# Ten expert weight pieces in idle buffers outside the ring, and a norm scale moved from rows to the copies out of PSUM

## The chip, the cores and the metric

One core of a Trainium2 chip runs the whole program as one launch. The metric is device microseconds (us) of one execution. TensorE (PE) does the matmuls and transposes, VectorE (DVE) and ScalarE (ACT) the elementwise work, GpSimd (POOL) a little of it and most of the small DMAs, and the queue of SyncE (SP) issues every weight transfer.

## The reference, cut to what matters

Everything is fp32, 512 tokens of width 1024. A first block (attention of two kinds, then a mixture of 32 experts) ends in a norm, and a second block of two layers begins with another norm of the same rows:

```python
def rmsnorm(x, g):                       # rms_norm is the same
    return x * rsqrt(mean(x * x, -1) + EPS) * g

h2 = rmsnorm(x, norm_ffn_g)              # first block, second half
for e in range(32):                      # every token takes 2 of 32 experts of one group
    hid = silu(h2 @ w_gate[e]) * (h2 @ w_up[e])
    m += (hid @ w_down[e]) * combine[:, e:e + 1]
x = rmsnorm(x + m, final_norm_g)         # end of the first block

h = rms_norm(x, norm_gain[0])            # second block, layer 0
cols = h @ w_in_a                        # q, k, v (3 x 3072), q_mem (512), gate (1536)
# q and k are normed for each head of 128, v is used as it is, silu(gate)
mem_out = cross attention of q_mem (normed) over kv = rmsnorm(mem) @ w_mem_kv[0]
```

Two row scales are thus applied one after the other: `both_rs[:, 0:4]` (final norm) and the second norm's, and `n2_rs` is their product, one number for each token. A scale of a row of x is also a scale of the same row of x @ w.

## The kernel before, in words

**Weights.** All weights come as `pieces` of up to 128x1024 fp32 (512 KB), in one fixed order. SP's `load(p)` (L633) puts piece p into slot p % 6 of the ring `wraw` once the low half of piece p - 6 has been made (L635). ACT's `feed(p)` (L864) copies it into a rounded high half `whi` (L869; the slot is one of four, and free when piece p - 4 has been used), DVE's `feed(p)` makes the low half `wlo` = raw - high (L1434), and PE multiplies in three passes (high by high, high by low, low by high), six matmuls of up to 512 columns for each token tile and piece. All engines run programs written out by hand; semaphores tie them together, and each engine works strictly in its own order.

**Experts.** Pieces P0, P1, ... (counted from `P_MOE`) are those of the experts: four gate/up pieces and two down pieces for each of 32 experts, 192 in all, in the order gate/up of expert n, then down of expert n - 1. Tokens are gathered group by group (eight groups of four experts, 128 rows each) by an indirect DMA of POOL (`gather`, L779), transposed (`columns`), multiplied (`gate_up` L2561, `down` L2584), added to the gathered rows (`expert_sums`, L1876) and scattered back (L790). Ahead of it come the router's logits, ranks and `slot_from`, which the first gather waits for (DVE, L1786 to L1846). DVE makes the low half of the last piece before the experts (`after(CH["out1"])`) in the middle of that routing, and SP's load of P5 waits for it.

**The end of the first block.** PE puts the last group's rows back with `last_mm` (L2650, eight products of 512 columns, two PE instructions each), DVE adds them to x1 (`x_sum`, L1933) and multiplies a copy by the final gain (`x_gain`, L1935, into `xn`), ACT squares both (L1261), DVE and ACT make the scales (L1937 to L1943), and DVE (three tiles, L1946) and ACT (one, L1267) write the scaled rows into x1. PE transposes x1 (`memory_stage`, L2238), in an order that puts token 4p + r at column p of tile r. ACT and DVE split the transposed rows into `AT_hi` and `AT_lo`. PE's `memory_stage(0)` runs four tiles of `mkv01` (values of the memory, which don't need x) before it waits for the scaled rows and four among the transposes, then `qm0` (q_mem, four pieces by four tiles, 96 matmuls), the head norms' transposes and the memory attention. POOL multiplies `xn` by the final scale and writes it to `x_mid` for the residual (L814, L815).

**Layer 0 of the second block.** For each of eight heads (`hd`) three chunks q, k, v of 384 columns run beside the attention of the head before, step by step (i = 0 to 11). At the end of a q or k chunk, for each of four tiles: ACT squares the PSUM bank (L1307), DVE sums the squares (L2007) and multiplies the bank by the head gain (L2009), which frees the bank for PE's next chunk; ACT's next square waits for DVE's sum. A v chunk is copied out by ACT (L1303), and the gate goes through Silu (L1028).

Of the kernel before, what the change touches and what calls it, by code (L numbers as in the profile page):

```python
# [20 lines left out]
ALU = mybir.AluOpType  # L21
# [83 lines left out]
def build(nc, A, out):  # L105
    ctx = ExitStack()
    with ctx:
# [29 lines left out]
        x_mid2 = nc.dram_tensor("x_mid2", (T, D), F32, kind="Internal").ap()  # L137

# [37 lines left out]
        gains = take(64)  # L176
        g_moe = gains[:, 53:61]
# [117 lines left out]


# [41 lines left out]
        raw_in = [S(f"raw_in{i}") for i in range(RAW)]  # L338
        hi_done = S("hi_done")
# [64 lines left out]
        sqrt_ready = stat(1)  # L404
        far_at = stat_at[0]
# [30 lines left out]
        before, iota_g, iota_s, empty, tok1 = (const(k, c_moe, C_BASE) for k in ("before", "iota_g", "iota_s", "empty", "tok1"))  # L436
        h2T = take(4096, KD, T)
# [21 lines left out]
        fin_g = take(D)  # L459
        big = take(4096)  # L460
# [19 lines left out]
        put = take(T)  # L480
        gen_sil = take(1024, 2, T)
# [18 lines left out]
        assert mem_at >= moe_top  # L500
        memx = [view(mem_at, 2048, 2, D), take(2048, 2, D)]
# [125 lines left out]
        @block.sync  # L627
        def _(sp):
            for t in range(NT):
                sp.dma_start(xr[:, t, :], A["x"][0, t * P:t * P + P, :]).then_inc(S(f"x_in{t}"), 16)  # L630

            def load(p):
                loads, per, n = pieces[p]  # L633
                if p >= RAW:
                    sp.wait_ge(lo_done[(p - RAW) % SPL], (p - RAW) // SPL + 1)  # L635
                dst = wraw[:, p % RAW, 0:per * n].rearrange("p (k n) -> p k n", k=per)
                share = 96 // len(loads)
                for c0, w, src in loads:
                    sp.dma_start(dst[:, :, c0:c0 + w], src).then_inc(raw_in[p % RAW], share)

            for p in range(NP):
                load(p)

        NORMS = (("n1", 4, 0, 0), ("cq", 4, 0, 0), ("ckv", 4, 0, 0), ("mem0", 2, 2, 0), ("ffn", 8, 0, 0),
                 ("n2", 8, 4, 0), ("km0", 0, 8, 2), ("qm0", 0, 0, 4), ("mem1", 2, 2, 0), ("n3", 4, 4, 0), ("km1", 0, 8, 2),
# [5 lines left out]
        def so_far(name, what, n):  # L653

            return sum(row[what] for row in NORMS[:ORDER.index(name)]) + n

# [31 lines left out]
        def _(pool):  # L688
# [64 lines left out]
            for p in BESIDE_PICKS:  # L753
                pool.wait_ge(hi_done, p + 1)
                pool.tensor_tensor(w_slot(wlo, p, p % SPL), w_slot(wraw, p, p % RAW), w_slot(whi, p, p % SPL).bitcast(F32),
                                   ALU.subtract).then_inc(lo_done[p % SPL], 1)
# [53 lines left out]

            pool.wait_ge(norm_rt, ORDER.index("n2") + 1)
            pool.wait_ge(norm_xs, so_far("n2", 2, NT))
# [46 lines left out]
        def _(act):  # L859
            his = [0]  # L860

            def feed(p):

                if p >= NP:  # L864
                    return
                act.wait_ge(raw_in[p % RAW], 96 * (p // RAW + 1))
                if p >= SPL:
                    act.wait_ge(piece_used, p - SPL + 1)
                act.activation(w_slot(whi, p, p % SPL), w_slot(wraw, p, p % RAW), ACT.Copy).then_inc(hi_done, 1)  # L869
# [8 lines left out]
            def evac(name, dst, func=ACT.Copy, scale=1.0, fed=False, rows=None):  # L878
# [4 lines left out]
                for t in range(chunks[j]["nt"]):  # L883
# [5 lines left out]
                    act.activation(d, src, func, scale=scale if rows is None else ns[rows]["rs"][:, t:t + 1]).then_inc(acc_free[t], 1)  # L889
# [14 lines left out]
            def tb(name, i):  # L904
                return TP[(TPU[name] + i) % 2]
# [94 lines left out]
            def memory_stage(l):  # L1000
# [3 lines left out]
                for k in range(KD):  # L1004
                    hi(name, k, AT_hi[:, k, :], tb(name, k), g_n2[l][:, k:k + 1])
                    if k % 2:
                        feed(chunks[j]["first"] + k // 2 + SPL)
                evac(f"mkv{l}1", lambda t: vm[l][:, t, :], fed=True)
                head_norm(f"km{l}", f"mkv{l}0", km_tok[l], 2, ns[f"km{l}"], msq)
                evac(f"qm{l}", lambda t: qm_tok[:, t, :])  # L1010
# [6 lines left out]
            def gate_out(l, c, tmp):  # L1017

                j = CH[f"gate{l}{THIRDS[l][c]}"]
                for t in range(NT):  # L1020
# [7 lines left out]
                    act.activation(tmp[n % len(tmp)], ACC[t][:, :], ACT.Silu).then_inc(acc_free[t], 1)  # L1028
# [10 lines left out]
            for at, src in ((0, A["norm_mix_g"][0]), (8, A["mla_q_norm_g"][0]), (11, A["mla_kv_norm_g"][0]), (13, A["norm_ffn_g"][0]),  # L1039
                            (21, A["norm_gain_2"][0]), (29, A["norm_gain_2"][1]), (37, A["mem_norm_gain_2"][0]),  # L1040
                            (45, A["mem_norm_gain_2"][1])):
# [10 lines left out]
            act.activation(gains[:, 0:53], SC[0][:, 0:53], ACT.Copy).then_inc(S("gains_ready"), 1)  # L1052
# [203 lines left out]
            done = so_far("n2", 1, 0)  # L1256
            for t in range(NT):
                for what, src, ss in (("x_sum", x1[:, t, :], fin_ss), ("x_gain", xn[t], n2_ss)):
                    act.wait_ge(S(what), 2 * t + 2 if what == "x_sum" else t + 1)
                    act.wait_ge(norm_ss, done)  # L1260
                    act.activation(junkD, src, ACT.Square, accum_out=ss[:, t:t + 1]).then_inc(norm_ss, 1)  # L1261
                    done += 1
# [3 lines left out]
            act.wait_ge(S("n2_rs"), 1)  # L1266
            act.activation(x1[:, 3, :], xn[3], ACT.Copy, scale=n2_rs[:, 3:4]).then_inc(norm_xs, 1)  # L1267
# [7 lines left out]
            for hd in range(9):  # L1275
                for i in range(12):
# [1516 lines left out]
```

## Time and profile before

| | |
|---|---|
| three runs | 2171.64, 2175.24, 2175.42 us, median 2175.24 |
| the profiled execution | 2176.21 us, of which the span is 2174.4 us |
| TensorE | 93% busy, mean granted clock 0.976 |
| chain that ended last | PE 71%, DVE 12%, ACT 8%, DMA 5%, issue 3% |
| DMA | 255.46 MB, mean 117 GB/s |

The span is what the profile covers, from the first to the last instruction. A matmul's end is modelled, so neighbouring matmuls overlap in the lists; the distance from start to start is their pace. A table row in square brackets ends with the idle time before the group and what ended it.

### The profile page before, as it was taken

What the parts mean: (1) busy time and instruction counts of PE and PEld (TensorE: products, weight loads), DVE (VectorE), ACT (ScalarE), POOL (GpSimd) and SP (SyncE); (2) the same over time, 40 slices, a digit from 0 to 9 for tenths busy, and PEclk for the clock granted to TensorE, in tenths of its full rate; (3) what the DMA queues carried; (4) which work ended last, traced back from release to release, by engine and by line L of the source; (5) the groups of instructions that cost most, each with busy time, mean ns of one, the idle gap of its engine ahead of it and who ended that gap; (6) DMA issues with size and microseconds to landing.
All of it is one profiled execution on the core that took longest, in us unless ns stands there. A gap on an engine that the chain in (4) does not pass through costs nothing.

```text
span 2174.4 us, 28065 instructions
## 1 busy us (share of the span) xinstructions
PE 2020.1 (93%) x10543; PEld 1707.1 (79%) x10543; DVE 1175.6 (54%) x2428; ACT 1032.7 (47%) x1705; POOL 243.7 (11%) x345
## 2 busy tenths in 40 slices
PE   7999999999899997799999999999999899998988
PEld 7977667777777775699988898888777677877877
DVE  3344387454899997454344334443433546736752
ACT  4644433344778786553444344434432554344430
POOL 0611132011010100212120112111000000000000
PEclk9999999999999999899999999999999999999999
DMA  4411121143899998322222222222243312112120
GB/s 141 134 47 40 58 70 57 39 146 140 284 373 362 373 368 309 97 63 74 66 72 59 73 66 66 66 74 86 68 129 116 116 55 78 30 49 78 49 88 39
DMA packets 177985, 255.46 MB, mean 117 GB/s; under 512 B 13557, under 2 KB 92218, under 8 KB 177850
## 3 DMA queue, kind: packets, MB, share of 16 engines
q1 hardware_dynamic: 168832, 221.33, 31.3%
q0 software_dynamic: 8768, 31.81, 4.0%
q8 instruction: 85, 1.39, 0.3%
q10 hardware_dynamic: 250, 0.52, 0.1%
q14 instruction: 50, 0.41, 0.1%
HBM read 239.45 MB, written 14.16 MB: 117 GB/s over the span
## 4 chain that ended last, share of the span: by engine, by line
PE 71%; DVE 12%; ACT 8%; DMA 5%; issue 3%; ACTq 0%; SPq 0%; POOL 0%; DVEq 0%; POOLq 0%
PE pb L2212 51%; DVE wlo L1434 5%; PE pb L2240 5%; DMA wraw<-w_down 5%; ACT whi L869 3%; PE pb L2744 3%; PE pb L2676 2%; PE pb L2292 2%; PE pb L2667 2%; PE pb L2305 1%; PE pb L2561 1%; PE pb L2584 1%; PE pb L2448 1%; PE pb L2753 1%; PE pb L2256 1%
## 5 line engine op out<-in xcount | busy, mean ns | idle before, releaser
L1434 DVE TENSOR_TENSOR wlo<-wraw,whi 128x1024 fp32r<-128x1024 f32 (+4 forms) x436 | 497.6, 1152 | 588.4 <-ACT whi L869 585.1
L2212 PE MATMUL pb<-whi,AT_hi 128*128 128x512 f32 (+4 forms) x1992 | 768.4, 386 | 22.7 <-ACT arena L889 5.8
L2212 PE MATMUL pb<-whi,AT_lo 128*128 128x512 f32 (+4 forms) x1992 | 730.8, 367 | 0.0
L2212 PE MATMUL pb<-wlo,AT_hi 128*128 128x512 f32 (+4 forms) x1992 | 730.2, 367 | 0.0
L869 ACT ACTIVATE whi<-wraw 128x1024 fp32r<-128x1024 f32 (+4 forms) x452 | 446.5, 996 | 477.3 <-PE pb L2212 403.6
L2212 PEld LDWEIGHTS pb<-whi,AT_hi 128*128 128x128 f32 x1992 | 380.4, 191 | 97.8 <-issue 44.3
L2212 PEld LDWEIGHTS pb<-whi,AT_lo 128*128 128x128 f32 x1992 | 378.7, 190 | 46.1
L2212 PEld LDWEIGHTS pb<-wlo,AT_hi 128*128 128x128 f32 x1992 | 380.7, 191 | 39.1 <-issue 2.5
L2240 PE MATMUL pb<-arena 128*128 128x128 f32 (+1 forms) x1180 | 188.9, 288 | 48.3 <-ACT arena L902 15.4
L2240 PEld LDWEIGHTS pb<-arena 128*128 128x128 f32 (+1 forms) x1180 | 147.8, 149 | 89.4 <-ACT arena L902 23.2
L2561 PE MATMUL pb<-whi,AT_hi 128*128 128x512 f32 x256 | 104.2, 407 | 4.3 <-DVE wlo L1434 2.3
L2561 PE MATMUL pb<-wlo,AT_hi 128*128 128x512 f32 x256 | 101.3, 396 | 0.0
L2561 PE MATMUL pb<-whi,AT_lo 128*128 128x512 f32 x256 | 100.8, 394 | 0.0
L2744 PEld LDWEIGHTS pb<-arena 128*128 128x128 f32 x576 | 78.4, 201 | 18.1 <-issue 10.7
L2744 PE MATMUL pb<-arena 128*128 128x64 f32 (+2 forms) x576 | 82.0, 290 | 10.7 <-DVE arena L2124 4.2
L1374 ACT ACTIVATE arena<-arena 128x512 f32<-128x512 f32 x64 | 40.3, 631 | 92.1 <-DVE arena L2110 74.8
L957 ACT ACTIVATE arena<-pb,small 128x64 f32<-128x64 f32 x64 | 20.1, 314 | 115.2 <-PE pb L2305 115.2
L902 ACT ACTIVATE arena<-pb 128x512 f32<-128x512 f32 (+2 forms) x102 | 55.3, 574 | 35.9 <-PE pb L2240 35.9
L703 POOL TENSOR_TENSOR arena<-arena 128x64 f32<-128x64 f32 (+3 forms) x41 | 18.3, 446 | 461.1 <-DVE small L2021 300.4
L2584 PE MATMUL pb<-whi,AT_hi 128*128 128x512 f32 x128 | 52.6, 411 | 16.7 <-DVE AT_lo L1868 13.0
L1283 ACT ACTIVATE arena<-arena,small 128x768 f32<-128x768 f32 x32 | 30.0, 939 | 66.9 <-DVE small L1982 66.9
L2561 PEld LDWEIGHTS pb<-whi,AT_hi 128*128 128x128 f32 x256 | 48.8, 191 | 14.7 <-DVE wlo L1434 3.0
(302 smaller groups left out, 2313.2 us busy)
## 6 DMA issues: line engine op xcount, KB each, us to landing
wraw<-w_in_a SPq DMA_DIRECT2D x288, 128.0 KB
wraw<-w_gate SPq DMA_DIRECT2D x128, 256.0 KB
wraw<-w_up SPq DMA_DIRECT2D x128, 256.0 KB
wraw<-w_down SPq DMA_DIRECT2D x64, 512.0 KB
wraw<-w_in_b SPq DMA_DIRECT2D x40, 512.0 KB
wraw<-w_in SPq DMA_DIRECT2D x28, 512.0 KB
wraw<-w_mem_kv SPq DMA_DIRECT2D x16, 512.0 KB
wraw<-w_in_a SPq DMA_DIRECT2D x16, 512.0 KB
```

The lines of the kernel that those rows point to most:

```text
L869: act.activation(w_slot(whi, p, p % SPL), w_slot(wraw, p, p % RAW), ACT.Copy).then_inc(hi_done, 1)
L902: act.activation(dst, src, ACT.Copy, scale=scale).then_inc(tp_free[u % 2], 1)
L1374: act.activation(kq[n % 5], kq[n % 5], ACT.Exp).then_inc(S("gl_x"), 1)
L1434: dve.tensor_tensor(w_slot(wlo, p, p % SPL), w_slot(wraw, p, p % RAW), w_slot(whi, p, p % SPL).bitcast(F32), ALU.subtract).then_inc(lo_don ...
L2212: mm = pe.matmul(ACC[t][:, 0:n], a, b, start=kc == 0 and q == 0, stop=i == c["count"] - 1 and kk == per - 1 and q == 2)
L2240: tr = pe.transpose(TP[u % 2][0:b.shape[1], at:at + P], b, ident)
L2292: pe.matmul(SC[U % 2][:, 0:u["kw"]], u["q"], u["k"], start=True, stop=True).then_inc(att_s, 1)
L2561: mm = pe.matmul(ACC[n % 2].rearrange("p (w f) -> p w f", w=2), a, b, start=k == 0 and m == 0, stop=k == 7 and m == 2)
L2584: mm = pe.matmul(ACC[2 + i], x, y, start=e == 0 and b == 0 and q == 0, stop=e == 3 and b == 1 and q == 2)
L2667: mm = pe.matmul(dst[:, 0:k.shape[1]], q, k, start=True, stop=True)
L2676: mm = pe.matmul(D_OUT, d_pt[:, P * b:P * b + P], v, start=b == 0, stop=b == 5)
L2744: mm = pe.matmul(dst, tile(k, s), rhs, start=True, stop=True)
```

## The change

(1) Pieces P6 to P15 (`HELD`) don't go into the ring: each has a buffer of its own, in regions of the arena that are unused until after the experts, and a semaphore of its own. Their loads wait for events that come before P5's load; the ring counts on without them, so P16 takes the slot that P6 had. (2) PE transposes x1 as it is after `x_sum`, beside the last `mkv01` tiles; the final gain is folded into the gain column of the transposed rows (`g_n2[0]`, DVE, once at the start, from one more small load). The squares and the scales are made beside it. `n2_rs` goes through DRAM (one write and one read of 512 numbers by POOL) to come back as `rs_perm` in the order of the transposed tiles, and every copy out of PSUM of layer 0 that reads x's columns takes it as its scale: `qm0` (ACT), the squares and the v copies (ACT), the product with the head gain (DVE, now `scalar_tensor_tensor`) and the Silu (ACT).

```diff
+        NHELD = 10
+        HELD = range(P_MOE + RAW, P_MOE + RAW + NHELD)
+        ring_at = lambda p: p if p < HELD.start else p - NHELD
+        ring_piece = lambda r: r if r < HELD.start else r + NHELD
...
+        held = [view(at + 1024 * i, 1024) for at, n in ((mem_at + 2304, 2), (gen_at, 2), (big_at + 2048, 2), (h2_at, 4)) for i in range(n)]
...
-                if p >= RAW:
-                    sp.wait_ge(lo_done[(p - RAW) % SPL], (p - RAW) // SPL + 1)
+                if p in HELD:
+                    i = p - HELD.start
+                    if i == 0:
+                        sp.wait_ge(S("y_sum"), 2 * NT)
+                    elif i == 2:
+                        sp.wait_ge(norm_ss, so_far("mem0", 1, 2))
+                    elif i == 4:
+                        sp.wait_ge(norm_ss, so_far("ffn", 1, 8))
+                    elif i == 6:
+                        sp.wait_ge(S("rt_mm"), 1)
+                elif ring_at(p) >= RAW:
+                    before = ring_piece(ring_at(p) - RAW)
+                    sp.wait_ge(lo_done[before % SPL], before // SPL + 1)
...
+            pool.wait_ge(S("n2_rs"), 1)
+                pool.dma_start(rs_rows.rearrange("(t p) -> p t", p=P), n2_rs).then_inc(S("rs_out"), 16)
+                pool.wait_ge(S("rs_out"), 16)
+                pool.dma_start(rs_perm, rs_rows.rearrange("(p r) -> p r", r=4)).then_inc(S("rs_back"), 16)
             pool.wait_ge(norm_rt, ORDER.index("n2") + 1)
-            pool.wait_ge(norm_xs, so_far("n2", 2, NT))
...
+                if l == 0:
+                    during(CH["qm0"])
+                    act.wait_ge(S("rs_back"), 16)
+                evac(f"qm{l}", lambda t: qm_tok[:, t, :], fed=l == 0, row_scale=None if l else rs_perm)
...
+            square_of(0)
+            square_of(1)
+            for k in range(KD):
+                hi("n2", k, AT_hi[:, k, :], tb("n2", k), g_n2[0][:, k:k + 1])
+                if k in (1, 3):
+                    feed(chunks[j]["first"] + k // 2 + SPL)
+                if k == 5:
+                    for t in range(2):
+                        wait_acc(act, j, t)
+                        act.activation(vm[0][:, t, :], ACC[t], ACT.Copy).then_inc(acc_free[t], 1)
+                        feed(chunks[j]["first"] + 2 + t + SPL)
+            for n in range(2, 8):
+                square_of(n)
...
-                                act.activation(v2[:, hd % 2, t, :], ACC[t][:, 0:384], ACT.Copy).then_inc(acc_free[t], 1)
+                                act.activation(v2[:, hd % 2, t, :], ACC[t][:, 0:384], ACT.Copy, scale=rs_perm[:, t:t + 1]).then_inc(acc_free[t], 1)
...
-                                act.activation(sqb, ACC[t][:, 0:384], ACT.Square).then_inc(S("qk_sq"), 1)
+                                act.activation(sqb, ACC[t][:, 0:384], ACT.Square, scale=rs_perm[:, t:t + 1]).then_inc(S("qk_sq"), 1)
...
-            for t in range(3):
-                dve.tensor_scalar(x1[:, t, :], xn[t], n2_rs[:, t:t + 1], None, ALU.mult).then_inc(norm_xs, 1)
...
-                            dve.tensor_tensor(qk_t[:, t, :].rearrange("p (g c) -> p g c", g=3),
...
+                            dve.scalar_tensor_tensor(qk_t[:, t, :].rearrange("p (g c) -> p g c", g=3),
+                                                     ACC[t][:, 0:384].rearrange("p (g c) -> p g c", g=3), rs_perm[:, t:t + 1],
+                                                     qkg[:, :, i // 4, :], ALU.mult, ALU.mult).then_inc(acc_free[t], 1)
...
-            memory_stage(0, lambda t: x1[:, t, :], lambda bank, t: bank.rearrange("p (r t q) -> p t q r", t=NT, r=4)[:, t], 4)
+                if t:
+                    project_tile("mkv01", (t - 1) // 2, (t - 1) % 2)
+            project_tile("mkv01", 1, 1)
+            pe.wait_ge(S("x_sum"), 8)
...
+            n2_t(0)
+            n2_t(1)
+            for s in range(4):
+                project_tile("mkv01", 2 + s // 2, s % 2)
+                n2_t(2 + s)
+            for i in range(4):
+                ready("n2", (2 * i, 2 * i + 1))
+                for t in range(NT):
+                    project_tile("qm0", i, t)
+                    if i == 0 and t % 2:
+                        n2_t(6 + t // 2)
+            memory_attention(0)
```

DVE's order becomes: all `x_sum` adds, the eight low halves of the transposed rows, then the four `x_gain` products and the scales.

## Rows read from the trace of the kernel before

**Rows 1.** The page: GB/s of all DMA in 40 slices of 54.4 us.
```profile
GB/s 141 134 47 40 58 70 57 39 146 140 284 373 362 373 368 309 97 63 74 66 72 59 73 66 66 66 74 86 68 129 116 116 55 78 30 49 78 49 88 39
```

**Rows 2.** Timeline of SP's queue, 530 to 562: start, duration, engine, line, operation.
```profile
537.15 0.35 SPq L639 DMA_DIRECT2D wraw<-w_gate  x1
541.31 0.35 SPq L639 DMA_DIRECT2D wraw<-w_gate  x1
```

**Rows 3.** Waits, 575 to 598, longest first: us in total, times, longest.
```profile
ACT whi L869 <- PE pb L2561: 1.7, 6, 0.3
```

**Rows 4.** Waits, 540 to 900.
```profile
ACT whi L869 <- DMA wraw<-w_up: 20.0, 21, 2.7
PE pb L2584 <- DVE AT_lo L1868: 13.0, 15, 2.7
ACT whi L869 <- DMA wraw<-w_down: 10.1, 29, 1.8
```

**Rows 5.** Timeline of POOL: scatters of the first and second group.
```profile
599.73 1.17 POOL L790 DMA_INDIRECT x_moe<-arena  x1 [56.23 <-DVE arena L1876]
636.57 1.71 POOL L790 DMA_INDIRECT x_moe<-arena  x1 [28.70 <-DVE arena L1876]
```

**Rows 6.** The chain that ended last, in order of time, 500 to 960: start, us, what.
```profile
540.65 5.87 DMA arena<-x_all,arena
...
602.33 6.75 DMA wraw<-w_down
...
892.58 23.41 PE pb L2212 x96
```

**Rows 7.** DMA issues, 675 to 685: us from issue to landing.
```profile
arena<-x_all,arena POOLq DMA_INDIRECT x1, 8.2
```

**Rows 8.** Timeline of PE, 855 to 935: start, duration, and idle time before.
```profile
860.30 7.14 PE L2650 MATMUL pb<-arena 128*128 128x512 f32 x16 [1.71 <-DVE arena L1908]
...
876.89 1.12 PE L2238 MATMUL pb<-arena 128*128 128x128 f32 x4 [4.00 <-DVE arena L1946]
...
892.58 0.77 PE L2212 MATMUL pb<-whi,AT_hi 128*128 128x512 f32 x1 [2.30 <-ACT arena L889]
...
915.82 0.60 PE L2240 MATMUL pb<-arena 128*128 128x128 f32 x4
```

**Rows 9.** A window of 5 us: busy us of PE, PEld, DVE, ACT, POOL; clock, DMA.
```profile
875.00:880.00 5.00, 3.11 (x10) 2.63 (x11) 2.59 (x4) 1.60 (x2) 2.85 (x1) 0.50 0.00 0
```

**Rows 10.** Timeline of DVE and ACT, 855 to 935.
```profile
870.43 1.22 DVE L1935 TENSOR_TENSOR arena<-arena 128x1024 f32<-128x1024 f32 x1
...
874.56 0.16 DVE L1943 TENSOR_TENSOR small<-small 128x4 f32<-128x4 f32 x1 [0.62 <-ACT small L1265]
...
871.76 1.06 ACT L1261 ACTIVATE arena<-arena 128x1024 f32<-128x1024 f32 x1
...
916.02 0.60 ACT L889 ACTIVATE arena<-pb 128x512 f32<-128x512 f32 x1 [0.76 <-PE pb L2212]
```

**Rows 11.** DMA issues of POOL: KB each, us from issue to landing.
```profile
arena<-const POOLq DMA_DIRECT2D x1, 134.5 KB, 2.4
arena<-lb_logits POOLq DMA_DIRECT2D x2, 4.0 KB, 4.3
...
x_mid<-arena POOLq DMA_DIRECT2D x4, 512.0 KB, 3.7
```

**Rows 12.** Groups of ACT by form: busy us, mean ns; a source `small` is a scale column.
```profile
L1303 ACT ACTIVATE arena<-pb 128x384 f32<-128x384 f32 x32 | 15.7, 492 | 18.4 <-PE pb L2212 18.4
L889 ACT ACTIVATE arena<-pb,small 128x384 f32<-128x384 f32 x8 | 4.3, 581 | 0.6 <-PE pb L2212 0.6
```

**Rows 13.** Waits of PE, 947 to 1500.
```profile
PE pb L2676 <- DVE arena L1989: 9.0, 7, 1.3
PE pb L2667 <- ACT arena L1303: 5.3, 7, 0.8
```

**Rows 14.** Timeline, the first 22 us: the gains' transpose.
```profile
9.84 0.32 PE L2374 MATMUL pb<-arena 53*128 53x53 f32 x1 [9.84 <-DMA arena<-mem_norm_gain]
```

More of the change, by code:

```diff
@@ L338, in build @@
         raw_in = [S(f"raw_in{i}") for i in range(RAW)]
+        raw_held = [S(f"raw_held{i}") for i in range(NHELD)]
         hi_done = S("hi_done")
@@ L404, in build @@
         sqrt_ready = stat(1)
+        rs_perm = stat(4)
         far_at = stat_at[0]
@@ L624, in build, with so_far @@
         block = ctx.enter_context(nc.Block())
+        NORMS = (("n1", 4, 0, 0), ("cq", 4, 0, 0), ("ckv", 4, 0, 0), ("mem0", 2, 2, 0), ("ffn", 8, 0, 0),
+                 ("n2", 8, 0, 0), ("km0", 0, 8, 2), ("qm0", 0, 0, 4), ("mem1", 2, 2, 0), ("n3", 4, 4, 0), ("km1", 0, 8, 2),
+                 ("qm1", 0, 0, 4))
+        ORDER = [n[0] for n in NORMS]
+        norm_ss, norm_ms, norm_rt, norm_xs = S("norm_ss"), S("norm_ms"), S("norm_rt"), S("norm_xs")
+        head_sq, head_red = S("head_sq"), S("head_red")
+        def so_far(name, what, n):
+            return sum(row[what] for row in NORMS[:ORDER.index(name)]) + n
         @block.sync
@@ L876, in after, with evac @@
                 feed(chunks[j]["first"] + chunks[j]["count"] - 1 + SPL)
-            def evac(name, dst, func=ACT.Copy, scale=1.0, fed=False, rows=None):
+            def evac(name, dst, func=ACT.Copy, scale=1.0, fed=False, rows=None, row_scale=None):
                 j = CH[name]
@@ L888, in evac @@
                         src = src.rearrange("p (h c) -> p h c", h=d.shape[1])
[L889 removed]
+                    if rows:
+                        row_scale = ns[rows]["rs"]
+                    act.activation(d, src, func, scale=scale if row_scale is None else row_scale[:, t:t + 1]).then_inc(acc_free[t], 1)
                 if not fed:
@@ L1027, in gate_out @@
                         act.wait_ge(S("gated0"), n - 1)
-                    act.activation(tmp[n % len(tmp)], ACC[t][:, :], ACT.Silu).then_inc(acc_free[t], 1)
+                    act.activation(tmp[n % len(tmp)], ACC[t][:, :], ACT.Silu, scale=1.0 if l else rs_perm[:, t:t + 1]).then_inc(acc_free[t], 1)
             def gated_hi(l, c):
@@ L1254, in _, with square_of @@
                     act.activation(gen_sil[:, 1, :], ACC[1], ACT.Silu).then_inc(S("gen_silu"), 1)
[L1256 to L1262, printed above, removed]
+            def square_of(n):
+                t = n % NT
+                src, ss = ((x1[:, t, :], fin_ss), (xn[t], n2_ss))[n // NT]
+                act.wait_ge(S("x_gain"), t + 1) if n >= NT else act.wait_ge(S("x_sum"), 2 * t + 2)
+                act.wait_ge(norm_ss, so_far("n2", 1, n))
+                act.activation(junkD, src, ACT.Square, accum_out=ss[:, t:t + 1]).then_inc(norm_ss, 1)
+            j = CH["mkv01"]
+            square_of(0)
+            square_of(1)
+            for k in range(KD):
+                hi("n2", k, AT_hi[:, k, :], tb("n2", k), g_n2[0][:, k:k + 1])
+                if k in (1, 3):
+                    feed(chunks[j]["first"] + k // 2 + SPL)
+                if k == 5:
[5 more added lines that the diff above has]
+                square_of(n)
             act.activation(sqrt_ready, ns["ffn"]["ms"][:, 0:1], ACT.Sqrt)
@@ L1599, in memory_stage @@
                 j = CH[f"mkv{l}1"]
-                for k in range(KD):
+                for k in range(KD) if l else ():
                     lo(name, k, AT_lo[:, k, :], tb(name, k), AT_hi[:, k, :], g_n2[l][:, k:k + 1])
@@ L1933, in _ @@
                     dve.tensor_tensor(x, LAST[(2 * t + i) % 4], x, ALU.add).then_inc(S("x_sum"), 1)
+            j = CH["mkv01"]
+            for k in range(KD):
+                lo("n2", k, AT_lo[:, k, :], tb("n2", k), AT_hi[:, k, :], g_n2[0][:, k:k + 1])
+                if k in (1, 3):
+                    feed(chunks[j]["first"] + k // 2 + SPL)
+                if k == 5:
+                    for q in (2, 3):
+                        feed(chunks[j]["first"] + q + SPL)
+            for t in range(NT):
                 dve.wait_ge(S("x_sum"), 2 * t + 2)
@@ L2328, in memory_stage, with memory_rows @@
             def memory_stage(l, rows, place, before):
+                if l:
+                    memory_rows(l, rows, place, before)
+                memory_attention(l)
+            def memory_rows(l, rows, place, before):
                 name = f"n{l + 2}"
```

70 lines of the change are left out of this document (39 added, 31 removed).

## The prediction

> **What bounds the kernel now.** I read the chain of waits in order of time first, then the GB/s slices, then waits and timelines of three stretches. In the expert stage (552 to 860 us) the slices show 362 to 373 GB/s [rows 1], and the chain runs over weight transfers and over the gather that opens the stage [rows 6]. ACT waits 30.1 us for weights (20.0 + 10.1), of which some reaches PE: it stands 13.0 us ahead of the down products for their split input [rows 4]. That looks like a stage that wants more prefetch. But from 575 to 598 us, the time of the first group of experts, the longest of ACT's waits for a copy is on PE, and no DMA is in the list's head [rows 3]: the weights fall behind only afterwards. Around 870 us the stage's end is bound by latency: PE stands 4.00 us for DVE's scaled rows, runs at half clock (0.50 in 875 to 880), and stands 2.30 us more for ACT's copy of the mkv01 banks [rows 8, 9]. Layer 0's heads are PE's own work, except at the end of a q chunk, where PE waits for DVE 7 times, 9.0 us in all, and at v, where it waits for ACT's copies 7 times, 5.3 us [rows 13].
>
> **The held pieces.** P5 is issued at 537.15 and P6 at 541.31, four us later, when P0's low half is made [rows 2]. With the change P6 to P15 go out right behind P5: 5.2 MB, some 13 us at 400 GB/s, done by about 552. What follows is the point: P16 to P21 then fill the six ring slots, at the times at which P6 to P11 were loaded before, and P22 has to wait for the low half of P16, which is not made before about 578 us, after all held pieces are used. Between those times SP has nothing to issue. So the lead isn't carried: at 578 us the ring is full, in place of nearly full, and from there every load is released by the same low halves as before. The first group had no wait for weights anyway [rows 3]. The second group's wait is a load issued at 602.33 that takes 6.75 us [rows 6], well after the ring is back in its old rhythm. Groups come 36.84 us apart (599.73 to 636.57) [rows 5]; I give the held pieces -0.5 us, with 0 and -2 as ends for the second group.
>
> They cost something at the start. The first gather (issued 540.65) is on the chain and lands after 5.87 us with hardly a weight transfer beside it [rows 6]. Now ten pieces are in the queues at that moment. A gather in the full stage takes up to 8.2 us [rows 7]. That is 0 to +2.3 us on the chain, since PE does nothing else before its transposes; I take +1.4.
>
> **The end of the first block.** Before: last_mm starts at 860.30, qm0's 96 matmuls start at 892.58 and take 23.24 us to 915.82, the last copy of qm0 ends at 916.62 (916.02 + 0.60) [rows 8, 10]. After, on PE: last_mm 7.14; the eight mkv01 tiles of six matmuls, at qm0's full-clock pace of 0.227 us each (21.8 us for 96; the first few ran at half clock), 1.36 each, 10.9; six groups of transposes at 0.4, 2.4. That is 880.8. There PE waits for bank 0: ACT must split row 5 and copy the bank, about 1.6 us. Then qm0 21.8 and two transposes 0.8: PE is done at about 905.0, 10.8 us earlier. The 4.00 and most of the 2.30 us are gone and, without the long idle time, the half clock too.
>
> What is late next is the scale. ACT and DVE finish the eighth row's split at about 891; ACT then squares the remaining six (last two of them behind DVE's products), and the last square ends at about 898. From the last square's start to n2_rs takes 2.8 us before (871.76 to 874.56) [rows 10], so n2_rs is ready at about 899.6, 25 us later than before. Then come two DMAs in series. Nearest rows: a write to DRAM in this very stretch, 3.7 us for 512 KB; a load of 4 KB as single numbers, 4.3 us; the quickest of POOL, 2.4 us for 134.5 KB [rows 11]. I take 3.7 for the write and 4.3 for the read, as the nearest in kind, and 0.4 for POOL's and ACT's wakeups: rs_perm is there at 908.0. ACT's four copies (0.69 with a scale column, 0.1 overlapped) end at 910.4. That is 6.2 us before 916.62. What is queued behind ACT's wait is the last feed and the copies of the keys' transposes, and PE waits for those; they follow the copies as before. With 2.4 us for each DMA the copies are bound by PE and end at about 907.2 (-9.4); with 8.2 us, the slowest issue shown [rows 7], they end at 918.8 (+2.2). After 905 PE idles as it did before 924, so the half clock moves more than it goes: -0.5, ends -2 and +1. Together -6.7. DVE's and ACT's scaled rows (four) go with this; POOL's x_mid products start after its two DMAs, at about 904, take 15 us and are covered by the attention, which before ends at 946.
>
> The Trainium skill, "DMA: Bandwidth & Descriptors", section on the two cost components, gives a DMA a fixed cost of about 2.0 us and next to nothing for few bytes. By that rule the two would take 4.0 in place of 8.0 us, rs_perm would be there at 904, before PE is done, and this part would give about -9.9. The rows here, all above 2.4, don't bear that out for POOL's transfers, but they carry other traffic in front of them.
>
> **The scale column in layer 0.** The copy of a bank with a scale column takes 581 ns where one without takes 492, at 384 columns [rows 12]: +0.089 us for each. Where does it stand on the path? At the end of a q chunk PE reaches the next chunk and then the probabilities' product, which waits for DVE 7 times [rows 13]; that DVE work stands behind ACT's four squares, each released by DVE's sum of the one before, so a square's length adds in full: 4 x 0.089 = 0.36 for each of 7 heads, 2.5 us. At the end of a k chunk the squares start as soon as the first tile is complete and PE has a product to do first, so I count nothing; if they bind there too it is 8 x 0.36 = 2.9 more. v: PE waits for the last copy, 8 x 0.09 = 0.7. The gate's Silu, three chunks, 0.3. DVE's product grows too, from tensor_tensor to scalar_tensor_tensor; no row has it at 384 columns with a column scale from a PSUM bank, and I bound it by 0 and by 0.1 us a tile; it runs beside ACT's next square and is covered except for the last tile. Sum +3.5, ends 0 and +7.
>
> **The start.** PE's transpose of the gains waits for the last small load at 9.84 [rows 14]; one more load is issued ahead of it, 0.4 us by the spacing of the others, and x itself comes just behind. +0.3, ends 0 and +0.6. DVE's product of gains lies in idle time.
>
> **Sum.** -0.5 + 1.4 - 6.7 + 3.5 + 0.3 = -2.0. The profiled execution took 2176.21 us, the median is 2175.24; 2.0 less than the median is 2173.2. A difference under 0.2% (4.35 us) is about what a measurement of this kernel can't tell from none.
>
> **Rivals.**
> *The loads keep their lead.* If the ring's starvation is inherited from the cold start, the ten pieces take away most of what reaches PE, 13.0 less the 5 us of the last group, where x's return shares the DMA: -8. For it: the stage sits at its transfer rate [rows 1]. Against: the first group shows no such wait. 2173.2 - 7.5 = 2166.
> *The scale comes quickly.* Both DMAs near 2 us: -3.2 more, 2170, just outside "same".
> *The scale comes slowly (slower).* Place: ACT's wait for rs_back ahead of qm0's copies. Numbers of four bytes into DRAM and back, behind ACT, PE and then the whole attention. Price: every us beyond 905 + 3 of rs_perm; it decides from about 10 us for the two on (the part's gain is then no more than the 4.7 that the rest costs), and at 8.2 each the part is +1.7 in place of -6.7: 2173.2 + 8.4 = 2181.6.
> *The column binds everywhere (slower).* Squares at k as well and DVE's longer product in the chain: +3.5 more, with the gather at +2.3: 2178.
>
> **Chances.** The forecast 0.45, with its own range 2170.5 to 2177; quick scale 0.20; lead kept 0.12; slow scale 0.12; column everywhere 0.11. The range from 2165 to 2181 takes in the first four in most of their spread. Faster by over 0.2%: lead kept, most of quick scale and the forecast's edge, 0.36. Slower: slow scale and a part of the last case, 0.19. Same: 0.45.
>
> **What would show it.** SP's queue: ten loads between 538 and 550, then none between about 562 and 577; a first gather of 6.5 to 8 us; scatters still near 37 us apart, the first at 600 to 602. PE: qm0 starts near 883 without idle time of 4 us, at full clock. ACT: an idle stretch of a few us ahead of the first qm0 copy, released by a DMA, at about 908. L1307 at 580 ns, and 7 waits of L2676 each 0.3 us longer. It is wrong if scatters come under 36 us apart, if no wait for rs_back is seen, or if the heads' stage is not 2 to 5 us longer.

## The result, and the profile after

The changed kernel took 2180.82 us (median of 9, 2178.95 to 2188.01); the kernel before, beside it, 2175.24 (2171.16 to 2179.32). The ratio is 1.0034, 95% interval 1.002 to 1.0048: slower by some 7 us, where 2.0 us faster, 2173.2, was forecast (the two medians themselves are 5.6 us apart). The profiled execution took 2180.32 us, span 2178.6.

SP's queue does what the prediction said of it [rows 2]. Timeline of SP, after, 530 to 580:
```profile
537.95 0.65 SPq L687 DMA_DIRECT2D arena<-w_gate  x1
...
542.76 0.92 SPq L687 DMA_DIRECT2D arena<-w_down  x2
...
557.43 1.86 SPq L687 DMA_DIRECT2D wraw<-w_down  x2
575.49 0.35 SPq L687 DMA_DIRECT2D wraw<-w_gate  x1
```
The held pieces (written to `arena`) are all issued by 544, the ring is refilled by 559, and then nothing is issued for 16 us. What ACT and PE wait for in the stage is what it was [rows 4]. Waits, after, 540 to 900:
```profile
ACT whi L910 <- DMA wraw<-w_up: 19.5, 20, 2.8
PE pb L2659 <- DVE AT_lo L1930: 12.9, 15, 2.7
ACT whi L910 <- DMA wraw<-w_down: 10.7, 31, 1.5
```
The first gather is slower, 8.37 us against 5.87 [rows 6]. The chain and the timelines of PE and POOL, after:
```profile
537.72 8.37 DMA arena<-x_all,arena
```
```profile
546.14 1.98 PE L2308 MATMUL pb<-arena 128*128 128x128 f32 x8 [5.30 <-DMA arena<-x_all,arena]
```
```profile
598.60 1.17 POOL L827 DMA_INDIRECT x_moe<-arena  x1 [58.03 <-DVE arena L1938]
...
635.52 1.71 POOL L827 DMA_INDIRECT x_moe<-arena  x1 [28.59 <-DVE arena L1938]
```
The groups still come 36.9 us apart [rows 5]. At the end of the first block PE does what was forecast: no wait of 4.00 us, full granted clock in 875 to 880 where it was 0.50 [rows 8, 9], and it is done at 905.44 (forecast 905.0). The window of 5 us, and PE's timeline, after:
```profile
875.00:880.00 5.00, 5.00 (x30) 4.24 (x29) 4.01 (x5) 3.61 (x5) 0.00 (x0) 1.00 0.27 79
```
```profile
882.56 0.47 PE L2280 MATMUL pb<-whi,AT_hi 128*128 128x512 f32 x1 [1.36 <-ACT arena L1322]
...
905.44 0.60 PE L2308 MATMUL pb<-arena 128*128 128x128 f32 x4
918.27 5.15 PE L2308 MATMUL pb<-arena 128*128 128x128 f32 x20 [12.23 <-ACT arena L945]
```
Then it stands 12.23 us. ACT's copies wait 10.63 us for `rs_perm`, and POOL, which may issue the read only when the write has landed, stands 9.43 us for that. DVE, POOL and ACT, after:
```profile
898.85 0.16 DVE L2014 TENSOR_TENSOR small<-small 128x4 f32<-128x4 f32 x1 [0.62 <-ACT small L1328]
```
```profile
899.31 0.78 POOL L850 DMA_DIRECT2D rs_rows<-small  x1 [65.63 <-DVE small L2014]
909.51 0.54 POOL L852 DMA_DIRECT2D small<-rs_rows  x1 [9.43 <-DMA rs_rows<-small]
```
```profile
914.79 2.42 ACT L932 ACTIVATE arena<-pb,small 128x512 f32<-128x512 f32 x4 [10.63 <-DMA small<-rs_rows]
```
The copies end at 917.21 (914.79 + 2.42), against 916.62 before [rows 10]. The transfers' own list (us from issue to landing at the end) and a window of 6 us inside the wait:
```profile
x_mid<-arena POOLq DMA_DIRECT2D x4, 512.0 KB, 3.0
rs_rows<-small POOLq DMA_DIRECT2D x1, 2.0 KB, 9.9
small<-rs_rows POOLq DMA_DIRECT2D x1, 2.0 KB, 5.3
```
```profile
899.00:905.00 6.00, 6.00 (x29) 4.95 (x28) 4.73 (x15) 3.39 (x6) 0.78 (x1) 1.00 0.03 0
```
2 KB take 9.9 us while the DMA engines are 3% busy (last but one number) and move 0 GB/s; 512 KB to DRAM take 3.0 us a little later. So the 9.9 us aren't other traffic.

In layer 0, ACT's squares are as long as priced [rows 12], and PE's waits stand elsewhere than I put them [rows 13]. Groups of ACT by form, and waits of PE, 947 to 1500, after; the last line is the one of the kernel before that belongs to the last line of after:
```profile
L1368 ACT ACTIVATE arena<-pb,small 128x384 f32<-128x384 f32 x64 | 37.1, 580 | 45.9 <-DVE small L2075 34.2 <-PE pb L2280 11.6
L1364 ACT ACTIVATE arena<-pb,small 128x384 f32<-128x384 f32 x32 | 18.6, 582 | 16.4 <-PE pb L2280 16.4
```
```profile
PE pb L2771 <- DVE arena L2057: 8.9, 7, 1.3
PE pb L2762 <- ACT arena L1364: 6.0, 7, 0.9
PE pb L2280 <- DVE arena L2077: 1.8, 7, 0.3
```
```profile
PE pb L2212 <- DVE arena L2009: 0.4, 1, 0.4
```

To compare runs, whose start differs by up to 6 us before anything changed, I read four stretches off POOL's timeline of each profiled execution. A runs from the first gather's issue to the first scatter, and B from the first to the seventh scatter (most of the expert stage). C runs from the seventh scatter to POOL's first product of layer 0's k heads with their norm's scale; the block's end and the q and k chunks of the first head lie in it. D runs from there to POOL's eighth such product (seven heads). In us; "time" is the ratio to the kernel before, where it was timed:

| kernel | A | B | C | D | time |
|---|---|---|---|---|---|
| before | 59.1 | 223.3 | 163.1 | 494.3 | 1 |
| after | 60.9 | 224.5 | 163.0 | 497.9 | 1.0034 |
| e1 held pieces alone | 62.4 | 223.7 | 162.9 | 494.2 | 1.0013 |
| e2 norm's move alone | 59.5 | 224.6 | 164.1 | 497.8 | 1.0043 |
| e3 product, no transfers | 61.1 | 225.0 | 156.9 | 497.9 | 1.0006 |
| e4 no column on q, k | 60.6 | 226.3 | 163.4 | 495.0 | 1.0034 |
| e5 16-byte write | 61.1 | 224.1 | 155.2 | 497.8 | |
| e6 ACT's queue | 62.4 | 222.5 | 162.7 | 497.8 | |
| e7 held after the gather | 57.1 | 224.6 | 164.7 | 497.8 | 1.0010 |
| e8 repaired, nothing held | 59.5 | 223.8 | 154.4 | 495.0 | 0.9963 |
| e9, e13 spaced numbers | 62.7, 62.3 | 225.5, 224.4 | 154.3, 154.2 | 497.8 | 0.9993 (e13) |
| e10 8-byte write | 60.8 | 224.0 | 160.1 | 497.9 | |
| e11 = e8 + held late | 57.0 | 223.4 | 153.4 | 495.1 | 0.9959 |
| e12 = e11, 16-byte write | 57.2 | 223.9 | 154.5 | 495.0 | 0.9968 |
| e14 = e11, spaced numbers | 57.1 | 224.9 | 152.2 | 495.0 | 0.9945 |

D repeats within 0.1 us among kernels that don't differ there, A and C within some 2 us; B (222.5 to 226.3) follows none of the edits. The three kernels that hold nothing have a mean B of 223.9, the thirteen with held pieces 224.4. e5, e6, e9 and e10 are single executions, read for their traces and not for their time.

### The profile page after: what moved, and what is told of

Its sections match the earlier page's. It is cut to its first block, busy times and chain, and to the rows that moved or that the text cites. A ratio compares the mean times of both kernels' runs of the same rounds, so it can differ in the third digit from the quotient of the medians.

```text
span 2178.6 us, 28064 instructions
## 1 busy us (share of the span) xinstructions
PE 2016.2 (93%) x10543; PEld 1702.7 (78%) x10543; DVE 1176.3 (54%) x2426; ACT 1040.6 (48%) x1704; POOL 242.9 (11%) x347
## 4 chain that ended last, share of the span: by engine, by line
PE 70%; DVE 13%; ACT 8%; DMA 6%; issue 2%; ACTq 0%; SPq 0%; POOL 0%; DVEq 0%; POOLq 0%
PE pb L2280 50%; DVE wlo L1495 6%; DMA wraw<-w_down 5%; PE pb L2308 5%; ACT whi L910 3%; PE pb L2839 2%; PE pb L2771 2%; PE pb L2360 2%; PE pb L2762 2%; PE pb L2373 1%; PE pb L2659 1%; PE pb L2636 1%; PE pb L2523 1%; PE pb L2848 1%; ACT arena L945 1%
## 5 line engine op out<-in xcount | busy, mean ns | idle before, releaser
L1495 DVE TENSOR_TENSOR wlo<-wraw,whi 128x1024 fp32r<-128x1024 f32 (+4 forms) x426 | 484.7, 1148 | 581.5 <-ACT whi L910 577.9
L910 ACT ACTIVATE whi<-wraw 128x1024 fp32r<-128x1024 f32 (+4 forms) x442 | 435.9, 994 | 458.7 <-PE pb L2280 387.1
L2280 PEld LDWEIGHTS pb<-whi,AT_hi 128*128 128x128 f32 x1992 | 379.2, 190 | 99.6 <-issue 44.3
L1632 DVE COPY arena<-pb 128x128 f32<-128x128 f32 (+3 forms) x64 | 31.4, 491 | 52.7 <-PE pb L2308 52.1
```

Source lines behind the costliest of these rows:

```text
L910: act.activation(w_slot(whi, p, p % SPL), raw_slot(p), ACT.Copy).then_inc(hi_done, 1)
L1495: dve.tensor_tensor(w_slot(wlo, p, p % SPL), raw_slot(p), w_slot(whi, p, p % SPL).bitcast(F32), ALU.subtract).then_inc(lo_done[p % SPL], 1)
L2280: mm = pe.matmul(ACC[t][:, 0:n], a, b, start=kc == 0 and q == 0, stop=i == c["count"] - 1 and kk == per - 1 and q == 2)
```

## The experiments

**Each part alone.** e1 is the kernel before with `HELD` and the addresses of its pieces; e2 is the changed kernel with
```
-        NHELD = 10
+        NHELD = 0
```


> The kernel before with the ten held pieces alone, its norm as it was. My reading of the changed kernel: the held pieces cost the first gather (PE stood 5.3 us for it in place of 2.8, the stage began about 1.8 us later against its input) and give nothing back, since the queue of loads stands still from 560 to 575: +1.8 us, 2177.0; scatters 36.9 us apart. Rival A (the lead is worth something, and the slower end hides it): below 2173, scatters under 36.7 us apart. Rival B (the gather's delay is taken back by a later, fuller ring): 2175.2, no difference.

Measured: 2175.79 us, ratio 1.0013 (1.0000 to 1.0025); wait for the gather 5.37 us. A costs 3.3 us here, 1.8 in the changed kernel, and B, which varies by more than that from kernel to kernel, shows nothing given back, here or in the means. The first rival has nothing for it; the second isn't excluded by the time, but A and B don't bear its mechanism out.

> The changed kernel with no held pieces (their number set to 0), the norm's scale still on the PSUM copies. If the two parts add up: start +0.7, end of the first block -0.6, the heads' stage +4.1, some 2179.4, and the first gather's wait is 2.8 us again. Rival (the parts work on each other: held pieces or their loads are what makes the round trip of the scale through memory slow): the write of the 512 numbers takes under 5 us and the time falls to 2175. My theory has that write at 9 us or more here too.

Measured: 2182.15 us, 1.0043 (1.0030 to 1.0056); wait for the gather 3.25 us, and the write still holds POOL 9.6 us. The held pieces have no part in the slow write. The two parts' losses (0.13% and 0.43%) add up to more than the whole's 0.34%, but within the intervals.

**The scale without the transfers.** e3 puts this in the place of both DMAs (`of_four` and `in_four` are 0/1 masks summed from `ident`):
```
+            dve.tensor_tensor(spread_rs.rearrange("p (t j) -> p t j", t=NT), n2_rs.unsqueeze(2).broadcast_to([P, NT, 32]),
+                              of_four.unsqueeze(1).broadcast_to([P, NT, 32]), ALU.mult).then_inc(S("n2_rs"), 1)
...
+                        pe.matmul(SC[1][:, 0:4], spread_rs, in_four, start=True, stop=True).then_inc(S("rs_mm"), 1)
...
+                    act.activation(rs_perm, SC[1][:, 0:4], ACT.Copy).then_inc(S("rs_back"), 1)
```


> The changed kernel, but the scale gets to its new layout on the chip: DVE spreads the four columns over 128 (times a 0/1 mask), one TensorE product with a second 0/1 mask gives [128,4], ACT copies it. No transfer. Theory (the round trip of 512 four-byte numbers is the step that ate the gain): the scale is there at about 902, qm0's copies end at 905 to 906 in place of 917.2, all that follows moves up by some 11.5 us: 2169. Rival A (something else binds right behind, the preparation of layer 0's heads by POOL's loads or the attention's start): copies end at 906 but the heads begin less than 5 us earlier: 2176 or more. Rival B (my forecast's own size, 6.7 us in all against the kernel before): 2175.

Measured: 2174.86 us, 1.0006 (0.9996 to 1.0015), C 6.1 us shorter than in the changed kernel. The copies start 46.0 us after last_mm's start in place of 54.4, and what they wait for is no longer a transfer; ACT's timeline in e3:
```profile
902.73 0.21 ACT L953 ACTIVATE small<-small 128x8 f32<-128x8 f32 x1 [2.13 <-DVE small L1523]
902.84 2.30 ACT L905 ACTIVATE whi<-wraw 128x768 fp32r<-128x768 f32 x3
905.05 0.15 ACT L1052 ACTIVATE small<-pb 128x4 f32<-128x4 f32 x1
905.23 2.42 ACT L927 ACTIVATE arena<-pb,small 128x512 f32<-128x512 f32 x4
```
ACT reaches the copies only after the keys' norm and three weight pieces. The theory named the right step and took too much for it: what comes next is work on ACT and DVE. Part of that is the edit's own. The keys' root (L953) comes 43.5 us after last_mm's start, 41.4 in the changed kernel, since DVE's work ahead of it is longer in e3: the spread takes 1.13 us, and the keys' small operation takes 1.34 us where it took 0.17 (DVE in e3):
```profile
897.87 1.13 DVE L2014 TENSOR_TENSOR arena<-small,arena 128x128 f32<-128x128 f32 x1
...
901.35 1.34 DVE L1523 TENSOR_SCALAR small<-small 128x8 f32<-128x8 f32 x1
```

**Why the round trip is slow.** e5, e6, e9 and e10 are each an edit of the changed kernel's two DMAs. e5 has the write contiguous in each partition and the read scattered:
```
-                pool.dma_start(rs_rows.rearrange("(t p) -> p t", p=P), n2_rs)
+                pool.dma_start(rs_rows.rearrange("(p t) -> p t", p=P), n2_rs)
-                pool.dma_start(rs_perm, rs_rows.rearrange("(p r) -> p r", r=4))
+                pool.dma_start(rs_perm, rs_rows.rearrange("(j r t) -> t j r", r=4, t=NT))
```


> The changed kernel with the layout change moved from the write to the read: each partition writes its four numbers as 16 bytes next to each other (128 elements), and the read collects 512 elements of four bytes. Before: 512 elements of four bytes written, POOL stands 9.4 us for them; 128 of 16 bytes read, 5.3 us from issue to landing. Theory (the number of small elements is what costs, in whichever direction): the write falls to about 5 us, the read rises to 9 or more, the sum stays near 15. Rival A (writing four-byte elements to DRAM is what costs, and reading them doesn't): 5 + 5, the copies of qm0 end 4 to 5 us earlier. Rival B (a fixed price of a write that POOL issues after a long pause, whatever its shape): the write stays at 9 to 10.

Measured: the list of transfers, and POOL and ACT, in e5:
```profile
rs_rows<-small POOLq DMA_DIRECT2D x1, 2.0 KB, 1.7
small<-rs_rows POOLq DMA_DIRECT2D x1, 2.0 KB, 4.6
```
```profile
899.41 0.56 POOL L850 DMA_DIRECT2D rs_rows<-small  x1 [65.79 <-DVE small L2014]
901.40 1.61 POOL L852 DMA_DIRECT2D small<-rs_rows  x1 [1.43 <-DMA rs_rows<-small]
```
```profile
905.99 2.42 ACT L932 ACTIVATE arena<-pb,small 128x512 f32<-128x512 f32 x4 [0.56 <-DMA small<-rs_rows]
```
The write falls from 9.9 to 1.7 us; the read of 512 single numbers takes 4.6, no more than the changed kernel's read of 128 groups of four (5.3). I had thought that small elements cost in whichever direction: only writing them did. C is 7.8 us shorter than in the changed kernel.

e6 has ACT issue the same two transfers.

> The changed kernel with the same two transfers, element for element, issued by ScalarE and not by GpSimd: the write right after the root, the read ahead of the feeds of qm0. Theory (GpSimd builds the descriptors of its transfers itself, element by element, and the row of the trace for its issue, 0.78 us, shows only the start of that): on ScalarE's queue the write lands in under 4 us, the read in 3, the scale is there before PE is done (905) and the copies end at about 908. Rival (the four-byte elements cost the same in every queue): the write takes 9 us as before, the copies end at 917.

Measured in e6:
```profile
rs_rows<-small ACTq DMA_DIRECT2D x1, 2.0 KB, 10.5
small<-rs_rows ACTq DMA_DIRECT2D x1, 2.0 KB, 2.9
```
My theory of the descriptors falls for the write: it is as slow from ACT's queue. The read is quicker from there, 2.9 in place of 5.3 us, which no run explains. The copies start 52.2 us after last_mm's start in place of 54.4; C, at 162.7, doesn't resolve that.

e9 leaves number and size of the elements and moves their addresses apart:
```
-                pool.dma_start(rs_rows.rearrange("(t p) -> p t", p=P), n2_rs)
+                pool.dma_start(rs_rows.rearrange("(t p s) -> p t s", p=P, s=16)[:, :, 0], n2_rs)
-                pool.dma_start(rs_perm, rs_rows.rearrange("(p r) -> p r", r=4))
+                pool.dma_start(rs_perm, rs_rows.rearrange("(p r s) -> p r s", r=4, s=16)[:, :, 0])
```


> The changed kernel, its 512 four-byte numbers written 64 bytes apart and read back from there. So the number and size of elements is as in the changed kernel (9.4 to 9.6 us waited in three runs), only their addresses don't touch. Theory A (neighbouring numbers, written in pieces of four bytes, get in each other's way in memory): the write lands in 2 to 4 us. Theory B (each small write has its price, by number or by size): it stays at 9 to 10 us.

Measured in e9:
```profile
rs_rows<-small POOLq DMA_DIRECT2D x1, 2.0 KB, 2.2
small<-rs_rows POOLq DMA_DIRECT2D x1, 2.0 KB, 2.2
```
512 writes of four bytes, 64 bytes apart, land in 2.2 us; next to each other in 9.9. The edit spaces the read too, and that falls from 5.3 to 2.2. So number, size, queue or a pause ahead of the write don't make it slow by themselves; it is slow when four-byte numbers of different partitions lie side by side. Neighbours alone don't do it either, since the 16-byte groups of e5 lie side by side as well. No run tells whether it is the neighbours as such or that all 512 writes fall into 2 KB. e10 writes pairs:

> The changed kernel, the numbers written in pairs: 256 elements of eight bytes next to each other, and the read in two transfers of 256 four-byte elements each. 512 of 4 bytes took 9.9 us from issue to landing, 128 of 16 bytes 1.7 us. If the price goes with the number of elements, this write takes about 4.5 us (1.7 + 128 x 0.0214); if it goes with neighbours in one stretch of memory or with a size under some bound, it is nearer to one of the two ends: 2 or 9 us.

Measured: the write lands in 3.4 us, the two reads in 4.8 and 6.1, and ACT stands 6.55 us for them:
```profile
rs_rows<-small POOLq DMA_DIRECT2D x1, 2.0 KB, 3.4
```
That lies between the ends, and under the 4.5 of a price by number. Its time (2177.1, one run) says nothing of the write, since there are two reads in place of one.

e13 is e9, timed:

> The kernel with the four-byte numbers 64 bytes apart again, now timed. One trace had the write at 2.2 us from issue to landing in place of 9.9, and the stretch from the seventh scatter to the first k product of layer 0 at 154.3 us in place of 163.0. Theory: the time falls by 8 us against the changed kernel's 1.0034, to 0.9995 of the kernel before, with +3.5 of the column and +1.9 of the gather still in it. Rival (the trace's gain is given back later, as the product's version, 1.0006, might suggest): 1.001 or more.

Measured: 2173.36 us, 0.9993 (0.9980 to 1.0006), C 154.2. The time follows the trace, as expected: one edit of addresses is worth about 0.4%, and its interval doesn't touch the changed kernel's (1.0020 to 1.0048).

**The column.** e4:
```
-                                act.activation(sqb, ACC[t][:, 0:384], ACT.Square, scale=rs_perm[:, t:t + 1])
+                                act.activation(sqb, ACC[t][:, 0:384], ACT.Square)
-                        dve.tensor_scalar(qk_n["ms"], qk_n["ss"], 1.0 / HD, EPS, ALU.mult, ALU.add)
+                        dve.scalar_tensor_tensor(per_g(qk_n["ms"]), per_g(qk_n["ss"]), 1.0 / HD,
+                                                 eps_row.unsqueeze(2).broadcast_to([P, NT, 3]), ALU.mult, ALU.add)
```
`eps_row` is EPS / rs_perm², made once, and DVE's product with the gains is a tensor_tensor again.

> The changed kernel with its round trip through memory, but no scale column on the q and k banks: x*s/sqrt(m*s*s+eps) is written as x/sqrt(m+eps/(s*s)), so ACT squares and DVE multiplies the bank as the kernel before does, and eps/(s*s) is a column made once. v and the gate keep the column. Theory (ACT's four squares in a row are the path at a q chunk's end, 7 times): the heads' period goes from 71.8 back to about 71.35 us and the time falls by 3.3 us to 2177.5. Rival A (it is v's copies that cost, 0.5 us a head): no more than 1 us is gained. Rival B (the column binds at k too): -6 us, 2175.

Measured: 2179.62 us, 1.0034 (1.0023 to 1.0045), so the time doesn't fall as expected; D falls by 2.9 us, to 495.0. The time doesn't resolve 3 us in this run (its 11 executions spread over 10 us); the stretch, which repeats within 0.1, does. 0.7 us of v's copies remain.

**The gather.** e7 adds, for the second held piece,
```
+                    elif i == 1:
+                        sp.wait_ge(S("x_row_in0"), 16)
```


> The changed kernel, but the second to tenth held piece are issued only when the first gather has landed. Theory (ten pieces in the queues slow the gather by 2.3 us, which is on the path, and the lead that they give is not carried): PE's wait for the gather is 2.8 to 3.3 us again in place of 5.3, and the stage from the gather's issue to the first scatter is 59.3 us in place of 61.2: -1.9, time 2179. Rival (the pieces come too late for the first group now): a wait of ACT for held pieces between 555 and 575 us, no gain or a loss.

Measured: 2177.31 us, 1.0010 (1.0000 to 1.0020). PE in e7:
```profile
541.88 1.21 PE L2310 MATMUL pb<-arena 128*128 128x128 f32 x8 [1.77 <-DMA arena<-x_all,arena]
```
PE stands 1.77 us for the gather, and A is 57.1: less than in the kernel before, where P6 is issued 0.7 us behind the gather. In e7 P6 goes out 2.6 us ahead of it and nothing between its issue and its landing. No wait of ACT for held pieces appeared.

**Put together.** e8 is e3 + e4 with nothing held; e11 is e3 + e4 + e7; e12 and e14 take the written forms of e5 and e9 in place of the product.

> The norm's move in the form that the runs so far suggest: no held pieces, the scale's layout change by one small TensorE product, no scale column on q and k (eps divided by the square of the factor). Added up against the kernel before: end of the block -7.1 (measured from last_mm to layer 0's first product with the product in place of the transfers: 79.4 against 86.5 us), heads' q and k 0, v's copies +0.6, the rest of the first block 0: -6.5 us, a ratio of 0.997. Rival (parts of the gain are not additive, or the run-to-run spread of the expert stage hides it): 0.999 or more.

Measured: 2167.14 us, 0.9963 (0.9952 to 0.9975), as expected or a little better; the rival's 0.999 is out.

> The repaired version (scale by a small product, no column on q and k) with the ten held pieces, from the second on issued after the first gather. In the run with late held pieces alone PE waited 1.8 us for the gather and gather to first scatter took 57.1 us, against 59.1 to 59.5 without held pieces. Theory (no weight transfer beside the gather is worth 2 us): 2 us below the repaired version without held pieces, 0.9954 of the kernel before. Rival (the 57.1 was one run's luck): 0.9963, as that one.

Measured: 2164.36 us, 0.9959 (0.9944 to 0.9974). A is 2.5 us shorter than in e8, as the theory has it; the times of the two can't be told apart.

> As the last, but the scale goes through memory, written as 16-byte elements and read as four-byte ones (1.7 + 4.6 us in the run that did that alone). There qm0's copies began at 905.99, 0.56 us held by the transfer, in place of 905.23 with the product, but PE and DVE have nothing added. Theory: within 1 us of the last, either sign. Rival (GpSimd's and DVE's shared work slows the spread, 1.13 us for an operation of 128 columns): 1 to 2 us faster than it.

Measured: 2166.19 us, 0.9968 (0.9955 to 0.9981), not told apart from e11 either.

> Spaced numbers, no column on q and k, held pieces after the first gather. Theory: against the last one -3.0 (column) and -4 (gather, 61.2 to 57.1): 0.9963 of the kernel before, level with the version by a small product (0.9959). Rival (what the two small changes give is not additive with the faster end): 0.998.

Measured: 2161.79 us, 0.9945 (0.9930 to 0.9960) from five executions: by the ratios 12 us below the kernel before and 19 below the changed one, where 0.9963 was expected. C is the shortest of all, 152.2. The intervals of e11 and e14 overlap. In the traces the copies start 43.7 us after last_mm's start in e14 and 46.1 in e8 and e11, so two quick transfers beat the small product at that place.

## Why the prediction was wrong

**The step that failed** is "I take 3.7 for the write and 4.3 for the read": the two took 9.9 + 5.3 us from issue to landing. `rs_perm` was forecast for 908.0 and came at about 914.8; the copies ended at 917.21 in place of 910.4. These 6.8 us are most of the miss, which is 7.6 us between 2173.2 and 2180.82, and 9.4 by the ratio (-2.0 forecast, +7.4 measured). e13 shows that this step cost the time: with other addresses the two transfers take 2.2 + 2.3 us, and the ratio falls from 1.0034 to 0.9993. The rows I priced from [rows 11] write 512 KB in long rows and *read* single numbers; none of them writes single numbers side by side. I took 2.4 and 8.2, the quickest and the slowest row, as bounds for each transfer, and the write lay above both. The measured time lies inside the widest range (to 2181), but by its edge, on the other side of the kernel before, and outside the forecast's own 2170.5 to 2177. The rival with the slow scale had the mechanism, its place and nearly its time (8.2 each: 2181.6; here 9.9 and 5.3), at a chance of 0.12.

The rest of the block's end came out as forecast: PE was done at 905.44 (905.0), n2_rs came at 898.85 (899.6), the idle 4 us were gone, and the granted clock was 1.00 in 875 to 880 and from 895 to 910. Behind PE's wait of 12.23 us it was 0.50 from 915 to 920, where it was 1.00 before; the half clock moved there, as I said. From the copies' end to the end of C it is 68.9 us, 69.5 before, so the term of -0.5 held. Where the transfers are quick the copies begin at 905.99 (e5), and C is 8 to 9 us shorter than before (e5, e9, e13), of the size of the -9.4 and -9.9 that I gave for quick ones.

The Trainium skill, "DMA: Bandwidth & Descriptors", section on the two cost components, would price each transfer at its fixed cost of about 2.0 us. The rows of e9 (2.2 and 2.2) and the write of e5 (1.7) agree; the packed write (9.9) is five times that, and POOL's packed reads (4.6 and 5.3) are over twice that, so the rule fails for the very shapes that the change uses. (The prediction holds against the rule that all its rows are above 2.4; the quickest of them is 2.4 itself.) The Trainium skill, in "Collectives: The Full Stack", section "Rules for kernel authors", advises 32-byte alignment of buffers against read-modify-write in hardware, for collectives; eight four-byte neighbours share such a stretch and the spaced ones don't, which fits. But two 16-byte groups share one as well, and their write is quick (1.7). That it is this mechanism no run here shows, and the cause stays open below the level of the addresses.

**Held pieces.** -0.5 was 0 as far as B can tell: the queue of loads stands still as forecast, and B doesn't fall. **First gather.** +1.4 was +1.8 (A), with PE's wait 2.5 us longer; e7 shows that it is the transfers beside it. Over all kernels with the ten pieces at once the mean of A is 2.2 above that of the three without. **Column.** +3.5 over the stage: D, seven of eight heads, has +3.5. Its size was right and the place partly wrong. I had expected 0.3 us more at each wait for the probabilities [rows 13]; these are unchanged (8.9 us). It stands ahead of the k chunk's first product, which waits for the q bank that DVE frees after ACT's four squares. The waits show it with 1.8 us in place of 0.4, which is too little, since they count from a modelled end. From the transposes ahead of that product to the probabilities' product PE takes 7.37 us a head in place of 6.95 (7.24 in one head), and 6.95 again in e4: 0.42 for each of seven heads, the 2.9 us that e4 gives back. v has +0.7 as priced. **Start.** The gains' transpose waits until 10.49 in place of 9.84, but POOL's first rotation comes at 47.6 to 49.6 us in the kernels with that load and at 48.2 to 48.5 in the two without: +0.3 isn't seen, nor excluded.

Of the other rivals, loads that keep their lead (-8) would show in B, which doesn't fall, and a column that binds everywhere would put about 7 us in D, where 3.5 are.

By sum, with the measured stretches in place of my terms, A +1.8, C -0.1, D and the last head about +4 make 5.7, between the 5.6 us of the medians and the 7.4 of the ratio. B has +1.2 on top, which the other kernels show as spread. The two profiled executions are only 4.1 us apart, since the changed kernel reached its first gather 2.9 us earlier, before anything of weight differed; that too is spread (534.9 to 541.2 over all kernels).

## What to carry to other kernels

A round trip through DRAM of a few numbers can't be priced by its bytes: look at which addresses are written at the same time. If each partition writes single numbers, give each its own stretch of memory (64 bytes were enough, and the only spacing tried), or let each partition write its numbers side by side and scatter the read. And price an operation that the trace doesn't show with an upper end outside the rows, where its shape (small writes) isn't among them.

Held buffers gave nothing here, because the ring behind them was no deeper when they were used up; ask that first. A transfer that the chain waits for should be issued before the bulk loads, not behind them. A row's scale ahead of an RMS norm can be folded into its epsilon, x/sqrt(m+eps/(s*s)), which took the q and k columns' 2.9 us off seven heads.

## What the hardware did that I had not expected

512 four-byte numbers to DRAM: side by side 9.9 us (10.5 from ACT's queue), as 256 pairs 3.4 us, as 128 groups of four 1.7 us, single but 64 bytes apart 2.2 us. Reads show less of it: 512 single numbers took 4.6 us packed and 2.2 us spaced, and 128 groups of four 5.3 us from POOL's queue and 2.9 from ACT's; why is open. And PE's wait for a gather of 128 rows was 1.8 us with no weight piece issued while it ran, 2.8 to 3.3 with the ring's next piece issued behind it, and 5.1 to 6.1 with ten pieces issued around it.
